# First layer's output projection in three fp32r passes with its weights split on GpSimd, and the second layer's gate products stacked

## The chip, the cores and the metric
One core of one Trainium2 chip runs the kernel. The time is the device time of one execution in microseconds (us); the number given is the median over runs. The profile is of one execution, taken by the hardware profiler.

## The reference
A decoder trunk of two layers on 1024 tokens of width 1024, in fp32. What matters here, cut down:

```python
def even_layer(...):                       # layer 0
    cq, ckv, k_rope, g_mla, u, g_s5 = split(x @ w_in)
    o_mla = mla_attention(cq, ckv, k_rope, ...) * silu(g_mla)     # (1024, 512), 8 heads, causal
    o_s5 = s5_layer(u, ...) * silu(g_s5)                          # (1024, 256); its last step is
                                                                  # y * sigmoid(y @ w_glu + b_glu)
    return concatenate([o_mla, o_s5]) @ w_out                     # (1024, 768) @ (768, 1024)

def odd_layer(...):                        # layer 1
    q, k, v, gk_low, g = split(x @ w_in)                          # gk_low: 16 columns
    log_a = log_sigmoid(gk_low @ w_gk2 + b_gk) / 16               # w_gk2: (16, 512)
    return (gated_linear_attention(q, k, v, log_a) * silu(g)) @ w_out

for each layer:
    x = layer_norm(4 ** 0.25 * x + layer(x))
```

## The kernel before, in words
All five instruction streams are written out by hand: `sync` (SP) issues every DMA in one queue, and GpSimd (POOL), ScalarE (ACT), VectorE (DVE) and TensorE (PE) each run their list in order and wait on semaphores. `PsumPlan` hands out the eight PSUM banks: `claim` waits until the bank's last job is drained, `filled` and `drained` wait for a job's completion by TensorE and by its reader. The helper `group` (L1588) issues one accumulation of matmuls, `turned` (L1597) transposes on TensorE.

Two kinds of product are in use. A plain fp32 product is one `matmul` call, which the profile shows as two MATMUL records. For the large products the operands are split into hi (the value rounded to fp32r) and lo (the value less hi, as fp32r), and `split_pairs` makes three fp32r passes of each product: hi·hi, hi·lo and lo·hi. Splitting costs a copy into hi and a subtraction into lo. For weights both are done on GpSimd (`split`, L884 and L885, through `wqk_split_head` and `slice_split_at`).

Layer 0 goes through its input projections, the S5 branch and then attention. Attention is 64 steps, one for each of 8 query tiles (i) and 8 heads (h), tile by tile (`attention_steps`, L458 on). In step n TensorE transposes the probabilities of head n (into "pt" banks), computes the scores of a later step (four ahead for i under 4, else two) and the value product of step n-1. VectorE copies the transposed probabilities (L595), takes the later step's row maximum (L1423) and, at tile ends, normalises the output of the tile and multiplies it with its gate (L1466 to L1472). ACT computes the exponentials (L1063). GpSimd rotates the queries of each later tile (L600 to L605). In steps 44 to 59 VectorE also runs the 16 pieces of the S5 branch's sigmoid (`sigmoid_gate`, L1441 on): add one, reciprocal, multiply into gs5. The glu products that they need are done before attention.

Then comes the output stage: for each token tile i, `output(i)` multiplies the tile's 768 mixed channels (4 blocks of OT, 2 of gs5) with w_out0 into z0, two halves of 512 columns, 6 fp32 products each. The first tile's product stands right behind the last value product in TensorE's queue, and the turning of tile 7 (OT 7) behind that. `layer_norm` (L1194 on) on VectorE adds the residual, takes the statistics and, after a square root on ACT (L1087), normalises; GpSimd multiplies and adds the two LayerNorm vectors (L907, L908); TensorE transposes the result (`x1_turned`) one tile later than its product, ACT writes x1T_hi (L1094) and VectorE x1T_lo (L1488). w_out0 is one DMA (L745) into a tile that is free by then.

Layer 1 begins with `low_rank(n)` (16 columns of the input projection, in 3 x 8 fp32r passes for each half of the tokens), the first query/key head `queries_keys(0)` between the two, then `gate_z(m)` (plain fp32, 16 rows deep) and the other query/key products. ACT copies the low-rank result to gkT (L1090, L1098). The weights of query/key heads 0 and 1 are loaded (L751) during attention, after the last sigmoid gate, and split on GpSimd before the output stage.

## Time and profile before

| | us |
|---|---|
| median of 3 runs | 928.06 (923.01 to 928.16) |
| the profiled execution, its own time | 926.22 |
| its span in the trace | 924.5 |
| TensorE busy in the span | 892.7 |
| VectorE busy | 448.1 |
| ScalarE busy | 273.7 |
| GpSimd busy | 222.0 |

Times of instructions in the rows are from the start of the span. A row of the timeline has the start, the time that the merged instructions cover, the engine, the line, the operation, its output and inputs, the shape and the count; in brackets how long the engine had been idle and what ended that. MATMUL records overlap, so the pitch between starts says more than the duration of one.

### The profile page before, as it was taken

To read this page: it belongs to the slowest core of one execution; us is meant where nothing else is said; L and a number is where in the kernel's file an instruction comes from. 1 tells how busy PE (TensorE), PEld (TensorE's weight loads), DVE (VectorE), ACT (ScalarE), POOL (GpSimd) and SP (SyncE) were. 2 spreads that over 40 slices of the span, in tenths; PEclk is the share of its full clock that TensorE was granted. 3 is DMA by queue.
4 is the path that set the end of the run, shared out by engine and by line. 5 is a ranking of instruction groups with operands and counts; after the bars stand their busy time and mean duration, and the time that the engine had idled before them with its cause. 6 is when DMAs were issued, how large, how long until landed. Compare 5 with 4: busy or idle time off the path is not lost. (4 is left out here: it accounts for less than half of the span.)

```text
span 924.5 us, 11820 instructions
## 1 busy us (share of the span) xinstructions
PE 892.7 (97%) x4384; PEld 691.5 (75%) x4384; DVE 448.1 (48%) x787; ACT 273.7 (30%) x536; POOL 222.0 (24%) x245
## 2 busy tenths in 40 slices
PE   7999999999999999999998999999999999999995
PEld 6888776766788777744455877888888888888884
DVE  5988689456666898344440433100000025554453
ACT  6152414553433344211113445002020326211120
POOL 2000002411110100544443230033413333142243
PEclk9999999999999999999999999999999999999998
DMA  9010255220000000522213110021001332021111
GB/s 338 11 28 23 72 84 121 85 76 2 1 1 1 1 1 13 170 77 83 91 57 103 46 46 1 11 86 52 23 23 50 98 114 92 23 81 57 46 48 67
DMA packets 34888, 55.61 MB, mean 60 GB/s; under 512 B 7664, under 2 KB 21232, under 8 KB 34816
## 3 DMA queue, kind: packets, MB, share of 16 engines
q1 hardware_dynamic: 34832, 54.87, 19.5%
q8 instruction: 35, 0.57, 0.3%
q14 instruction: 21, 0.17, 0.1%
HBM read 43.78 MB, written 9.44 MB: 58 GB/s over the span
## 5 line engine op out<-in xcount | busy, mean ns | idle before, releaser
L1521 DVE SCALAR_TENSOR_TENSOR w_out_lo<-w_out_raw,vecs,w_out_hi 128x1024 fp32r<-128x1024 f32 x8 | 10.5, 1314 | 161.8 <-ACT w_out_hi L1131 161.6
L1812 PEld LDWEIGHTS psum<-V,probT 128*128 128x128 f32 x576 | 69.3, 192 | 11.7 <-issue 8.1
L1812 PE MATMUL psum<-V,probT 128*128 128x64 f32 x576 | 74.4, 275 | 0.3 <-DVE rot L1468 0.3
L1675 PE MATMUL psum<-kT,qTt 96*128 96x512 f32 (+3 forms) x192 | 72.5, 487 | 1.2 <-DVE YT L612 1.2
L1063 ACT ACTIVATE prob<-psum,negmax 128x128 f32<-128x128 f32 (+7 forms) x64 | 47.4, 740 | 81.6 <-DVE negmax L1423 71.0
L1423 DVE TENSOR_REDUCE negmax<-psum 128x1 f32<-128x128 f32 (+7 forms) x64 | 48.5, 758 | 29.8 <-PE psum L1679 28.4
L1588 PE MATMUL psum<-w_out,OT 128*128 128x512 f32 x128 | 57.6, 593 | 0.0
L1588 PE MATMUL psum<-x1T_hi,wqk_hi 128*128 128x512 f32 x128 | 51.2, 400 | 0.0
L1588 PE MATMUL psum<-x1T_lo,wqk_hi 128*128 128x512 f32 x128 | 50.8, 397 | 0.0
L1588 PE MATMUL psum<-x1T_hi,wqk_lo 128*128 128x512 f32 x128 | 50.6, 395 | 0.0
L1588 PE MATMUL psum<-w_out_hi,Y1T_hi 128*128 128x512 f32 x128 | 50.6, 395 | 0.0
L1588 PE MATMUL psum<-w_out_hi,Y1T_lo 128*128 128x512 f32 x128 | 49.9, 390 | 0.0
L1588 PE MATMUL psum<-w_out_lo,Y1T_hi 128*128 128x512 f32 x128 | 49.8, 389 | 0.0
L1623 PE MATMUL psum<-wg_hi,x1T_lo 128*128 128x512 f32 x128 | 49.8, 389 | 0.0
L1623 PE MATMUL psum<-wv_hi,x1T_hi 128*128 128x512 f32 x128 | 49.8, 389 | 0.0
L1623 PE MATMUL psum<-wv_lo,x1T_hi 128*128 128x512 f32 x128 | 49.8, 389 | 0.0
L1623 PE MATMUL psum<-wv_hi,x1T_lo 128*128 128x512 f32 x128 | 49.8, 389 | 0.0
L1623 PE MATMUL psum<-wg_hi,x1T_hi 128*128 128x512 f32 x128 | 49.8, 389 | 0.0
L1623 PE MATMUL psum<-wg_lo,x1T_hi 128*128 128x512 f32 x128 | 49.8, 389 | 0.0
L595 DVE COPY probT<-psum 128x512 f32<-128x512 f32 (+3 forms) x64 | 37.8, 591 | 20.6 <-PE psum L1597 18.8
L1675 PEld LDWEIGHTS psum<-kT,qTt 96*128 96x128 f32 x192 | 32.4, 190 | 20.0 <-issue 16.8
L1588 PEld LDWEIGHTS psum<-w_out,OT 128*128 128x128 f32 x128 | 23.7, 190 | 26.8 <-issue 26.8
(349 smaller groups left out, 1923.7 us busy)
## 6 DMA issues: line engine op xcount, KB each, us to landing
wqk_raw<-odd_w_in_dram SPq DMA_DIRECT2D x8, 512.0 KB, 5.3
x_res<-x_dram SPq DMA_DIRECT2D x8, 512.0 KB, 3.4
x_scratch<-zn SPq DMA_DIRECT2D x8, 512.0 KB, 2.6
wv_raw<-odd_w_in_dram SPq DMA_DIRECT2D x16, 256.0 KB, 2.7
wg_raw<-odd_w_in_dram SPq DMA_DIRECT2D x16, 256.0 KB, 2.7
w_out_raw<-odd_w_out_dram SPq DMA_DIRECT2D x4, 1024.0 KB, 5.0
V<-x_scratch SPq DMA_DIRECT2D x8, 512.0 KB, 4.2
out_dram<-SG SPq DMA_DIRECT2D x8, 512.0 KB, 2.9
```

The lines of the kernel that those rows point to most:

```text
L595: ins = engine.activation(dst, src, ACT.Copy) if engine is nc.scalar else engine.tensor_copy(dst, src)
L1063: step.frees(act.activation(prob[:, place:place + (i + 1) * P], src, ACT.Exp, bias=negmax[:, n % 4:n % 4 + 1], accum_out=rsum[:, i % 2, h: ...
L1423: step(vec.tensor_reduce(negmax[:, n % 4:n % 4 + 1], scores(n)[0], AX_X, ALU.max, negate=True), max_set)
L1521: step(vec.scalar_tensor_tensor(w_out1[2][:, k, :], w_out1[0][:, k, :], gla_c[:, 4 + k % 2:5 + k % 2], w_out1[1][:, k, :].bitcast(F32), AL ...
L1588: mm = pe.matmul(out, lhsT, rhs, start=(k == 0), stop=(k == len(pairs) - 1))
L1623: mm = pe.matmul(bank(*job)[:, c0:c1], lhsT, rhs, start=(k == 0 and j == 0 and c0 == 0), stop=(k == KD - 1 and j == len(pairs) - 1), skip_ ...
L1675: mm = pe.matmul(psum[:, slot + part, 0:c1 - c0], qTt[:, i % 2, h, :], kT[:, h, c0:c1], start=True, stop=not diag, skip_group_check=diag)
L1812: mm = pe.matmul(bank("o", i)[:, h * VD:(h + 1) * VD], lhsT, rhs, start=(k == 0), stop=(k == len(pairs) - 1))
```

## The change
1. Output projection: w_out0 is loaded in six slices of 128 rows (1 to 3 after the S5 products y are done on TensorE, 4 and 5 after the last sigmoid gate, 0 after the last query rotation) and split on GpSimd: slices 1 to 3 behind the rotations of tiles 2, 3 and 4, the others behind the last rotation. The mixed channels are split too, tile by tile: ACT writes mix_hi, VectorE OT_lo and gs5_lo. `output(i)` makes three fp32r passes of each of its 12 products, and waits for the tile's low part.
2. The sigmoid gates move from steps 44 to 59 to steps 8 to 23.
3. Gate products: w_gk2 is laid out six times below itself (96 rows). `low_rank` uses hi and lo of its weight side by side (32 output rows, 16 matmuls instead of 24), ACT and VectorE write the result in six stacked parts (low_parts), and `gate_z` is one fp32r pass, 96 rows deep.
4. Query/key head 1 is loaded and split only after the output stage. x_res and zn have other places; the first slices of v1 wait until the last z0 is drained. Some unused semaphores go.

```diff
             plan.filled(sp, ("y", 3))
-            sp.dma_start(w_out0[:, :, :], even_w_out[0].rearrange("(k p) n -> p k n", p=P)).then_inc(w_out0_loaded, 16)
+            for k in range(1, 4):
+                w_out0_load(k, 0)
...
             sp.wait_ge(s5_states_set, 4)
+            sp.wait_ge(s5_out_set, 16)
+            for k in range(4, 6):
+                w_out0_load(k, 1)
             plan.filled(sp, ("q", NT - 1, 1))
-            sp.wait_ge(s5_out_set, 16)
+            sp.wait_ge(q_turned, NT)
+            w_out0_load(0, 2)
             wqk_load(0)
-            wqk_load(1)
...
             plan.filled(sp, ("z0", NT - 1, 1))
+            wqk_load(1)
+            plan.drained(sp, ("z0", NT - 1, 1))
...
# gpsimd, behind the rotation of query tile i
+                if 2 <= i < 5:
+                    w_out0_split_slice(i - 1, 0, 48)
...
+            for k in range(4, 6):
+                w_out0_split_slice(k, 1, 32)
+            w_out0_split_slice(0, 2, 16)
             pool.wait_ge(wgk_loaded, 16)
-            split(*(t[:, :, :] for t in w_gk), wgk_split)
-            for h in range(2):
-                wqk_split_head(h)
+            split(w_gk_raw[:, :, :], w_gk[:, :, 0:GR], w_gk[:, :, GR:2 * GR], wgk_split)
+            wqk_split_head(0)
...
                 step(pool.tensor_tensor(z, z, ln_gb[:, 1, :], ALU.add), x1_set)
+                if i == 1:
+                    pool.wait_ge(small_loaded, 16 * 3)
+                    step(pool.tensor_copy(gk2_parts[:, :], gk2[:, :]))
+                    step(pool.tensor_tensor(gk2_parts[4 * GR:6 * GR, :], gk2[4 * GR:6 * GR, :],
+                                            gk2_parts[4 * GR:6 * GR, :].bitcast(F32), ALU.subtract), gk2_split)
+            wqk_split_head(1)
...
# scalar; for tile 0 at the end of attention, for tile 1 behind it, for i + 2 behind the root of tile i
+            def mix_hi_tile(i):
+                cols = slice(i * P, (i + 1) * P)
+                plan.drained(act, ("OT", i))
+                if i == 0:
+                    act.wait_ge(s5_out_set, 16)
+                if i >= 2:
+                    plan.filled(act, ("z0", i - 2, 1))
+                step(act.activation(mix_hi[i % 2][:, 0:4, :], OT[:, :, cols], ACT.Copy))
+                step(act.activation(mix_hi[i % 2][:, 4:6, :], gs5[:, :, cols], ACT.Copy), mix_hi_set)
...
+            def low_hi(n):
+                s = slice(n * 512, (n + 1) * 512)
+                plan.filled(act, ("gk", n))
+                step(act.activation(low_parts[0:2 * GR, s], bank("gk", n)[0:2 * GR, :], ACT.Copy))
+                step(act.activation(low_parts[4 * GR:6 * GR, s], bank("gk", n)[0:2 * GR, :], ACT.Copy), low_hi_set)
...
# vector; for tile 0 behind tile 7's gate, for tile 1 behind OT 7, for i + 2 behind layer_norm of tile i
+            def mix_lo_tile(i):
+                cols = slice(i * P, (i + 1) * P)
+                vec.wait_ge(mix_hi_set, i + 1)
+                step(vec.tensor_tensor(OT_lo[:, :, cols], OT[:, :, cols], mix_hi[i % 2][:, 0:4, :].bitcast(F32),
+                                       ALU.subtract))
+                step(vec.tensor_tensor(gs5_lo[:, :, cols], gs5[:, :, cols], mix_hi[i % 2][:, 4:6, :].bitcast(F32),
+                                       ALU.subtract), mix_split)
+            def low_lo(n):
+                s = slice(n * 512, (n + 1) * 512)
+                vec.wait_ge(low_hi_set, n + 1)
+                step.frees(vec.tensor_tensor(low_parts[2 * GR:4 * GR, s], bank("gk", n)[0:2 * GR, :],
+                                             low_parts[0:2 * GR, s].bitcast(F32), ALU.subtract), ("gk", n))
...
-                    if 44 <= n < 60:
-                        sigmoid_gate(n - 44)
+                    if 8 <= n < 24:
+                        sigmoid_gate(n - 8)
...
# tensor
             def output(i):
                 if i == 0:
-                    pe.wait_ge(w_out0_loaded, 16)
-                    pe.wait_ge(s5_out_set, 16)
-                plan.drained(pe, ("OT", i))
+                    pe.wait_ge(w_out0_split, MIX // P)
+                pe.wait_ge(mix_split, i + 1)
...
-                          [(OT[:, k, ts] if k < 4 else gs5[:, k - 4, ts], w_out0[:, k, cs]) for k in range(6)])
+                          split_pairs([((mix_hi[i % 2][:, k, :], OT_lo[:, k, ts] if k < 4 else gs5_lo[:, k - 4, ts]),
+                                        (w_out0_hi[:, k, cs], w_out0_lo[k][:, cs])) for k in range(6)]))
...
-                group(("gk", n), bank("gk", n)[0:GR, :],
-                      split_pairs([([w[:, k, :] for w in w_gk[1:]], [x_[:, k, n * 512:(n + 1) * 512] for x_ in x1T])
-                                   for k in range(KD)]))
+                group(("gk", n), bank("gk", n)[0:2 * GR, :],
+                      [(w_gk[:, k, :], x_[:, k, n * 512:(n + 1) * 512]) for k in range(KD) for x_ in x1T])
...
-                group(("gate", m), bank("gate", m), [(gk2[:, h * P:(h + 1) * P], gkT[:, n * 512:(n + 1) * 512])])
+                group(("gate", m), bank("gate", m), [(gk2_parts[:, h * P:(h + 1) * P], low_parts[:, n * 512:(n + 1) * 512])])
```

## Rows read from the trace of the kernel before

**Rows 1.** The page, busy time, share of the span and instructions by engine:
```profile
PE 892.7 (97%) x4384; PEld 691.5 (75%) x4384; DVE 448.1 (48%) x787; ACT 273.7 (30%) x536; POOL 222.0 (24%) x245
```
**Rows 2.** Busy time by stretch, two stretches of attention; clock, DMA share, GB/s last:
```profile
204.60:240.10 35.50, 33.21 (x206) 24.12 (x206) 24.25 (x46) 12.84 (x38) 5.67 (x13) 1.00 0.00 1
305.00:368.00 63.00, 63.00 (x417) 48.74 (x416) 57.92 (x90) 24.77 (x48) 1.29 (x4) 1.00 0.00 1
```
**Rows 3.** Timeline of TensorE, output stage, x1's transposes before two neighbouring tiles:
```profile
441.70 1.04 PE L1597 MATMUL psum<-ident,zn 128*128 128x128 f32 x8
...
452.87 1.04 PE L1597 MATMUL psum<-ident,zn 128*128 128x128 f32 x8
```
**Rows 4.** Timeline of TensorE, first query/key product's first pass, and what follows its last:
```profile
481.66 0.40 PE L1588 MATMUL psum<-x1T_hi,wqk_hi 128*128 128x512 f32 x1
...
492.57 1.03 PE L1597 MATMUL psum<-ident,zn 128*128 128x128 f32 x8
```
**Rows 5.** Timeline of VectorE, one sigmoid gate's first operation and what follows the gate:
```profile
305.61 0.23 DVE L1446 TENSOR_SCALAR SGL<-SGL 128x128 f32<-128x128 f32 x1
...
307.18 0.96 DVE L1423 TENSOR_REDUCE negmax<-psum 128x1 f32<-128x768 f32 x1
```
**Rows 6.** A weight split on GpSimd, VectorE's gate product beside it, and that line's durations:
```profile
383.89 1.04 POOL L884 CAST wqk_hi<-wqk_raw 128x1024 fp32r<-128x1024 f32 x1
385.01 2.35 POOL L885 TENSOR_TENSOR wqk_lo<-wqk_raw,wqk_hi 128x1024 fp32r<-128x1024 f32 x1
...
386.42 1.49 DVE L1472 TENSOR_TENSOR gate<-gate,rot 128x512 f32<-128x512 f32 x1
...
L1472 DVE TENSOR_TENSOR gate<-gate,rot x8: 693/693/1490, 207.9 to 386.4; 128x512 f32<-128x512 f32 x8
```
**Rows 7.** Timeline, start and end of the output stage, VectorE and then TensorE:
```profile
385.32 0.20 DVE L1466 RECIPROCAL rinv<-rsum 128x8 f32<-128x8 f32 x1 [3.27 <-PE psum L1812]
...
396.85 0.69 DVE L1199 SCALAR_TENSOR_TENSOR zn<-x_res,psum 128x512 f32<-128x512 f32 x1
...
402.30 0.81 DVE L1206 TENSOR_SCALAR zn<-zn,stat 128x1024 f32<-128x1024 f32 x1
403.15 0.69 DVE L1199 SCALAR_TENSOR_TENSOR zn<-x_res,psum 128x512 f32<-128x512 f32 x1
...
408.11 1.09 PE L1597 MATMUL psum<-ident,zn 128*128 128x128 f32 x8 [1.79 <-POOL zn L908]
...
475.22 1.04 PE L1597 MATMUL psum<-ident,zn 128*128 128x128 f32 x8
```
**Rows 8.** Timeline, output stage, one tile on VectorE and then on GpSimd:
```profile
419.64 0.69 DVE L1199 SCALAR_TENSOR_TENSOR zn<-x_res,psum 128x512 f32<-128x512 f32 x1 [3.66 <-PE psum L1588]
...
421.23 0.21 DVE L1203 BATCH_NORM_AGGREGATE stat<-stat 128x2 f32<-128x12 f32 x1
...
423.08 1.42 DVE L1488 TENSOR_TENSOR x1T_lo<-psum,x1T_hi 128x512 fp32r<-128x512 f32 x2
...
423.19 2.35 POOL L907 TENSOR_TENSOR zn<-zn,ln_gb 128x1024 f32<-128x1024 f32 x1 [8.41 <-DVE zn L1206]
425.62 2.36 POOL L908 TENSOR_TENSOR zn<-zn,ln_gb 128x1024 f32<-128x1024 f32 x1
```
**Rows 9.** Timeline of TensorE and one row of ACT, low-rank and gate products:
```profile
476.02 0.48 PE L1588 MATMUL psum<-x1T_hi,w_gk_hi 128*16 128x512 f32 x1
...
495.66 0.39 PE L1588 MATMUL psum<-x1T_hi,w_gk_hi 128*16 128x512 f32 x1 [2.06 <-DVE x1T_lo L1488]
...
501.31 3.14 PE L1588 MATMUL psum<-gkT,gk 16*128 16x512 f32 x6
...
506.65 0.80 PE L1588 MATMUL psum<-x1T_hi,wqk_hi 128*128 128x512 f32 x1
...
554.88 1.98 PE L1588 MATMUL psum<-gkT,gk 16*128 16x512 f32 x4
...
501.48 0.59 ACT L1098 ACTIVATE gkT<-psum 16x512 f32<-16x512 f32 x1 [6.99 <-PE psum L1588]
```
**Rows 10.** Busy time by stretch, as in rows 2, where the granted clock is lower:
```profile
506.60:511.50 4.90, 4.90 (x12) 3.81 (x12) 1.27 (x2) 3.37 (x3) 0.00 (x0) 0.50 0.00 0
```

More of the change, by code:

```diff
@@ L175, in hybrid_trunk @@
         gk2_at = cursor[0]
-        gk2 = own("gk2", [GR, GKW])
+        gk2 = own("gk2", [6 * GR, GKW])
         o = cursor[0]
@@ L265, in hybrid_trunk @@
         OT = at("OT", RB + 7424, [P, H * VD // P, S])
-        w_out0 = at("w_out0", RB, [P, MIX // P, D])
+        OT_lo = at("OT_lo", RB + 7424, [P, H * VD // P, S], F32R)
+        gs5_lo = at("gs5_lo", D6, [P, 2, S], F32R)
+        mix_hi = [at(f"mix_hi{s}", (RD + 8192, D5)[s], [P, MIX // P, P], F32R) for s in range(2)]
+        w_out0_hi = at("w_out0_hi", RB, [P, MIX // P, D], F32R)
+        w_out0_at = (RB + 6144, RT, RT + 1024, D1 + 2048, D7, D7 + 1024)
+        w_out0_raw = [at(f"w_out0_raw{k}", o, [P, D]) for k, o in enumerate(w_out0_at)]
+        w_out0_lo = [at(f"w_out0_lo{k}", o, [P, D], F32R) for k, o in enumerate(w_out0_at)]
         SGL = at("SGL", D7, [P, 4, 512])
@@ L294, in hybrid_trunk @@
         cum = at("cum", RD + 19456, [P, 2, 512])
-        w_gk = split_pair("w_gk", E2 + 4096, [P, KD, GR])
-        ends = at("ends", E2 + 4096 + 2 * KD * GR, [P, GH, NCH])
+        w_gk_raw = at("w_gk_raw", E2 + 4096, [P, KD, GR])
+        w_gk = at("w_gk", E2 + 4096 + KD * GR, [P, KD, 2 * GR], F32R)
+        ends = at("ends", E2 + 4096 + 3 * KD * GR, [P, GH, NCH])
         resets = at("resets", RD + 12288, [P, 512])
-        two_ends = at("two_ends", E2 + 4096 + 2 * KD * GR + 64, [P, GH, NT])
-        assert (E2 + 4096 + 2 * KD * GR + 96) * 4 <= nc.sbuf_usable_end - base
+        two_ends = at("two_ends", E2 + 4096 + 3 * KD * GR + 64, [P, GH, NT])
+        assert (E2 + 4096 + 3 * KD * GR + 96) * 4 <= nc.sbuf_usable_end - base
         w_out1 = (at("w_out1_raw", RC, [P, KD, D]), at("w_out1_hi", RA, [P, KD, D], F32R),
@@ L340, in hybrid_trunk @@
         q_turned = sem("q_turned")
-        max_set, prob_set = sem("max_set"), sem("prob_set")
+        max_set = sem("max_set")
         gated = sem("gated")
-        w_out0_loaded, ln0_loaded = sem("w_out0_loaded"), sem("ln0_loaded")
+        w_out0_loaded, ln0_loaded = [sem(f"w_out0_loaded{s}") for s in range(3)], sem("ln0_loaded")
+        w_out0_split, mix_hi_set, mix_split = sem("w_out0_split"), sem("mix_hi_set"), sem("mix_split")
+        gk2_split, low_hi_set = sem("gk2_split"), sem("low_hi_set")
         xres_loaded = [sem(f"xres_loaded{s}") for s in range(2)]
@@ L870, in _, with split, w_out0_split_slice @@
                          s5_states_set if table is tabB else None)
+            def split(raw, hi, lo, signal):
+                step(pool.tensor_copy(hi, raw))
+                step(pool.tensor_tensor(lo, raw, hi.bitcast(F32), ALU.subtract), signal)
+            def w_out0_split_slice(k, batch, landed):
+                pool.wait_ge(w_out0_loaded[batch], landed)
+                split(w_out0_raw[k][:, :], w_out0_hi[:, k, :], w_out0_lo[k][:, :], w_out0_split)
             pool.wait_ge(s5_n2_set, 4)
@@ L880, in _ @@
                            q_turned)
-            def split(raw, hi, lo, signal):
-                step(pool.tensor_copy(hi, raw))
-                step(pool.tensor_tensor(lo, raw, hi.bitcast(F32), ALU.subtract), signal)
+                if 2 <= i < 5:
+                    w_out0_split_slice(i - 1, 0, 48)
             def wqk_split_head(h):
@@ L1077, in _ @@
                     scaled_queries(*n)
+                elif what == "z0":
+                    mix_hi_tile(0)
                 elif what == "pt":
@@ L1087, in _ @@
                     step(act.activation(stat[:, 20:21], stat[:, 1:2], ACT.Sqrt, bias=eps[:, 0:1]), root_set)
+                if i + 2 < NT:
+                    mix_hi_tile(i + 2)
                 if i == NT:
-                    plan.filled(act, ("gk", 0))
-                    step.frees(act.activation(gkT[:, 0:512], bank("gk", 0)[0:GR, :], ACT.Copy), ("gk", 0))
+                    low_hi(0)
                 if i:
@@ L1096, in _ @@
                              x1_hi_set)
-            plan.filled(act, ("gk", 1))
-            step.frees(act.activation(gkT[:, 512:1024], bank("gk", 1)[0:GR, :], ACT.Copy), ("gk", 1))
+            low_hi(1)
             for h in range(GH + 1):
@@ L1288, in _ @@
             step(vec.tensor_tensor(LR[:, :, :], LR[:, :, :], e4[0], ALU.add))
-            step(vec.tensor_scalar(tabA[:, :, :], tabA[:, :, :], 1.0, None, ALU.add), s5_powers_set)
+            step(vec.tensor_scalar(tabA[:, :, :], tabA[:, :, :], 1.0, None, ALU.add))
             slice_lo("ina", 4)
@@ L1472, in _ @@
                     step(vec.tensor_tensor(gate[:, i, :], gate[:, i, :], rot[:, 0, :], ALU.mult), gated)
+                elif what == "z0":
+                    mix_lo_tile(0)
                 elif what == "OT":
@@ L1483, in _ @@
                     layer_norm(zn[:, i % 2, :], x_res[:, i % 2, :], "z0", i, i)
+                if i + 2 < NT:
+                    mix_lo_tile(i + 2)
                 if i:
@@ L1956 @@
     }
-    for name in ("mla_w_uq", "mla_w_ukv", "s5_w_glu", "even_w_out", "odd_w_in", "gla_w_gk2", "odd_w_out"):
+    laid_out["gla_w_gk2"] = np.tile(given["gla_w_gk2"][0], (6, 1))
+    for name in ("mla_w_uq", "mla_w_ukv", "s5_w_glu", "even_w_out", "odd_w_in", "odd_w_out"):
         laid_out[name] = given[name]
```

25 lines of the change are left out of this document (15 added, 10 removed).

## The prediction
> **What bounds the kernel now.** I read the page first, then TensorE's timeline and groups, then the same stretches on VectorE (DVE), ScalarE (ACT) and GpSimd (POOL). TensorE is the bound nearly throughout: 892.7 of 924.5 us busy [rows 1]. So what leaves its queue shortens the kernel, as long as no other engine takes over. Two stretches decide whether one does. In 305 to 368 us VectorE is 92% busy (57.92 of 63 us), and TensorE still has no gap [rows 2]: the sigmoid gates of the S5 branch sit there now and cost TensorE nothing. In 204.6 to 240.1 us (attention steps 8 to 23, where the gates go) VectorE has 24.25 of 35.5 us busy in 46 instructions [rows 2]: it looks half idle, but the steps are short. In the output stage TensorE runs one tile every 11.17 us (441.70 to 452.87), 0.87 of that transposes and 10.30 the products [rows 3].
>
> **Output projection, on TensorE.** One fp32 product appears as two records, and a tile has 12 products: 10.30/12 = 0.858 us each [rows 3]. The fp32r pitch is in the query/key products: 48 of them between 481.66 and 492.57, 0.227 us each [rows 4]. Three passes cost 0.68 us, so a tile falls to 12 x 0.68 = 8.18, plus 0.87 is 9.05 instead of 11.17 us. For eight tiles TensorE alone would give back 17.0 us.
>
> **The moved sigmoid gates.** One gate holds VectorE from 305.61 until the next operation at 307.18, 1.57 us [rows 5]; sixteen are 25.1 us. In their new place VectorE has 35.5 - 24.25 - 46 x 0.035 us between instructions (from 403.11 to 403.15, for one [rows 7]) = 9.6 us free. It runs in order, and its copy of the transposed probabilities is what the next value product waits for; behind each gate are queued that step's maximum (then the exponential, the next transposes) and the next copy. TensorE can run ahead by a step, not by sixteen. So 25.1 - 9.6 = 15.5 us comes onto the path. Bounds: 0 if all were hidden, 25.1 if none of the free time could be used; I take 15.5, because once VectorE has a backlog its short waits for TensorE go away. Taking the gates out of 305 to 368 gives nothing, since TensorE had no gap there.
>
> **Six weight splits on GpSimd.** Each is a cast of 1.04 and a subtraction of 2.35 us [rows 6]. GpSimd has the time; the three after query tiles 2 to 4 end long before the next rotation, and slices 4, 5 and 0 and the first query/key head fall at 306 to 330, before 385. What they cost is VectorE's time. The gate product of 128x512 took 1.49 us at 386.42, beside a subtraction that ran until 387.36; its median over eight is 0.693 [rows 6]. An operation with two SBUF inputs evidently waits until GpSimd's is over. The last multiplication of a sigmoid gate is of that kind, and there is one per 3.2 us (51 us over 16 steps): a subtraction meets one with 2.35/3.2 and holds it 1.2 us on average, the cast adds 0.17. Three splits: 3.2 us, and 0.3 for the query rotations. Bounds 0 and 3 x 3.39 = 10.2. I take 3.5; attention then grows by 19.0 us.
> The Trainium skill (SBUF — State Buffer, Who interferes with whom) says more than the row shows: tensor_scalar with one SBUF source can enter a two-port mode that takes the same lock, and the first to start holds it for the whole instruction. The gate's "+1" would then wait too. By the row the term is 3.5; by the rule about 2 us more. No row shows a tensor_scalar blocked, so it stays out of the sum.
>
> **The start of the output stage.** Now the first output follows the last value product at once, and tile 7's normalising runs beside it. With the change it waits for the low part of tile 0, which stands on VectorE behind tile 7's normalising. VectorE starts at 385.32 [rows 7]; reciprocal 0.31, product 0.79 and gate 0.73 (GpSimd is free now), then two subtractions, 0.73 and 0.42 (by 0.69 for 512 columns), end at 388.3. TensorE idles 3.3 us. Output 0 ends at 396.6, the turned tile 7 is copied by 398.0, tile 1's low part follows at 399.15: output 1 waits 2.2 us more. Normalising tile 0 took 396.85 to 403.11; from 399.15 it ends at 405.4. GpSimd's two operations follow (4.9 us, and 1.0 of blocking, below), so the first transposes of x1 start at 411.4 instead of 408.11 [rows 7].
>
> **The tiles after it.** VectorE does per tile: half a normalisation (1.59, from 419.64 to 421.23), a second half of 3.44 (419.64 to 423.08), and two x1 low parts, 1.42 and a gap [rows 8]. That was 6.5 of 11.17 us. New are two subtractions with two SBUF inputs, right where GpSimd starts on the tile (423.19) [rows 8]. The first (0.72) is ahead of GpSimd and delays it by 0.6; the second waits for GpSimd's first 2.35 us operation and then delays its second by 0.4. So mix_lo costs 0.72 + 2.35 + 0.43 = 3.5 us, VectorE's tile is 1.59 + 3.44 + 3.5 + 1.45 = 10.0, and that is more than TensorE's 9.05. Tile 1's normalising, started at 409.0, ends at 414.05, and each further tile 10.0 later: tile 6 at 464.05, its transposes 4.9 later at 469.0. Before, they started at 475.22 [rows 7]: the whole stage, start included, gains 6.2 us. Bounds: 10.6 at TensorE's own pace (411.4 less 1, then 6 x 9.05), and a loss of 3.3 if the pace stayed at 11.17.
>
> **The gate products.** The low-rank product falls from 24 to 16 matmuls of 0.233 us, twice (5.64 us for 24, from 476.02 to 481.66 [rows 4, 9]): 3.7 us. The four gate products after the second one run from 501.31 to 506.65, 5.34 us [rows 9]. In their place: two copies on ACT (0.59 each), one subtraction on VectorE (0.69), with handovers 2.4 us before the second product, and ACT must empty both banks for products 3 and 4: 3.9 us, 1.4 less. The four later ones cost 0.86 each (554.88, two in 1.9 us) [rows 9], now 0.23: 2.5. Together 7.6 us (bounds: 6.2 with no gain at the first four, 9.5 with all at pitch). The split of the 96-row weight (about 2 us) lies in GpSimd's gap after tile 1. The second query/key head now loads only after tile 7's x1 (477.4): 4 us of queue, 5 to land, 7 to split is 493.6, and its first product is due at about 506. This cover is 12 us wide.
>
> **TensorE's clock.** The granted clock is 1.00 in the attention stretches [rows 2], and 0.50 from 506.6 to 511.5 [rows 10], the lower level of 1.2 GHz, after 2.06 us idle before 495.66, narrow products and waits [rows 9]. There 12 products took 0.43 instead of 0.23 us, 2.4 us in all. I expect that one to stay. The new 3.3 us idle before output 0 may bring another: half of 2.4 is 1.2 us. Bounds 0 and 11.9: at the lower clock all through the starved stretch, its 33.2 us of TensorE work [rows 2] would take 66.4, against the 54.5 that VectorE needs.
>
> **Sum.** 19.0 - 6.2 - 7.6 + 1.2 = +6.4 us, on the profiled execution's own 926.22 (span 924.5 and 1.7 around it): 932.6 us. The median of the runs shown is 928.06, 1.8 above it; measured medians may stand as much higher.
>
> **The rivals.**
> (a) VectorE hides the gates, because 24.25 busy of 35.5 us [rows 2] leaves a third free. Then the change is faster: 926.2 - 6.2 - 7.6 + 1.2 = 913.6. Against it: 25.1 does not go into 9.6 us. It decides if VectorE's idle time in the stretch exceeds 25 us. Chance 0.07.
> (b) The blocking between VectorE and GpSimd is dear only by accident at 386 us; without it attention grows 15.5, and the output stage runs at TensorE's pace and gains 10.6: 926.2 + 15.5 - 10.6 - 7.6 + 1.2 = 924.7. For it: one blocked row only. Chance 0.17.
> (c) The clock falls in the starved stretch, where TensorE has work for 33 of 54 us. Work at half speed fills the gaps, and after a filled stretch the clock came back at 511.5, so I take half of the 11.9 us: 938.6. Against it: the same steps with less waiting run at 1.00 now. Chance 0.13.
> (d) The output stage keeps its old pace, because each tile waits for VectorE, ACT, VectorE, GpSimd in turn: 926.2 + 19.0 + 3.3 - 7.6 + 1.2 = 942.1. Against it: from the second half's start at 419.64 to x1 at 427.98 is 8.4 us [rows 8], under 9. Chance 0.11.
> My own forecast has 0.52, with 928 to 938 as its range.
>
> **How the numbers follow.** Time 932.6. The range takes in (b) and the two slower ones: 922 to 943. A measurement of this kernel can tell about 1% (9 us) from no change. Faster by more than that is (a), 0.07. Slower by more, over 935.5, is (c), (d) and a fifth of mine: 0.35. The rest, 0.58, is within 1%.
>
> **What would show it.** In the profile after: 16 reciprocals of 128x128 between 205 and 262 us, VectorE over 90% busy there, step 24 starting 17 to 22 us later than 240.1; some gate multiplications far over 0.29 us, one of 1.2 or more per split; TensorE idle 3 us before the first output; the output stage's period at 10.0 us, TensorE idle 1 us per tile on x1 or mix_lo; 32 low-rank matmuls; attention's end at about 404. I am wrong if step 24 starts before 250, if the period is 9.05, or if TensorE's clock leaves 1.00 before 385.

## The result, and the profile after

The kernel after takes 939.25 us (median of four runs, 936.33 to 943.81), the kernel before in the same job 927.27. The ratio is 1.0143, with a 95% interval of 0.0052 either way (1.0091 to 1.0195): slower by 1.4%. The forecast was 932.6 us with a range of 922 to 943, so the time lies inside, 6.65 us above the likeliest value. The profiled execution took 938.81 us, its span 937.1 against 924.5.

The page of the kernel after, its busy times and the granted clock in 40 slices:

```profile
PE 882.4 (94%) x4456; PEld 716.0 (76%) x4456; DVE 481.9 (51%) x805; ACT 283.4 (30%) x554; POOL 251.7 (27%) x259
...
PEclk9999999997699999999999899999999999999998
```

TensorE is busy 10.3 us less than before [rows 1], and the kernel is longer: it was made to wait. Two slices in the tenth and eleventh place stand at 7 and 6. That is attention, where the gates now are. Busy time by stretch there (from, to, length, then TensorE, its weight loads, VectorE, ScalarE, GpSimd, and the granted clock):

```profile
204.60:262.00 57.40, 43.24 (x201) 29.54 (x200) 48.27 (x86) 11.87 (x36) 15.78 (x19) 0.76 0.00 1
...
212.00:216.00 4.00, 1.99 (x4) 1.17 (x4) 3.76 (x8) 0.00 (x0) 0.00 (x0) 0.50 0.00 0
```

Before, TensorE was busy 33.21 of 35.5 us at 1.00 here [rows 2]. Now it has 43.24 of 57.4 at a mean of 0.76, and in 212 to 216 half of the time at 0.50 (1.2 GHz). Where it waits, TensorE's waits of the whole kernel (total, times, longest, us):

```profile
PE psum L1668 <- DVE qTt L1466: 9.3, 4, 3.4
...
PE psum L1883 <- DVE probT L602: 4.9, 4, 3.0
PE psum L1659 <- issue: 3.2, 1, 3.2
```

A line names the waiting engine and its line, and behind the arrow who ended the wait. The turned queries (qTt) and the turned probabilities (probT) are VectorE copies that stand behind a gate in its queue. The line "issue, 3.2" is the start of the output stage. TensorE's timeline from the last value product on (start, length, and in brackets the idle time before and who ended it):

```profile
407.91 3.68 PE L1883 MATMUL psum<-V,probT 128*128 128x64 f32 x32
...
414.76 0.47 PE L1659 MATMUL psum<-w_out_hi,mix_hi 128*128 128x512 f32 x1 [3.17 <-issue]
...
427.29 0.50 PE L1659 MATMUL psum<-w_out_hi,mix_hi 128*128 128x512 f32 x1 [2.04 <-DVE gs_lo L1505]
...
439.07 1.09 PE L1668 MATMUL psum<-ident,zn 128*128 128x128 f32 x8 [1.71 <-POOL zn L932]
...
467.20 1.09 PE L1668 MATMUL psum<-ident,zn 128*128 128x128 f32 x8 [0.43 <-POOL zn L932]
...
476.92 1.09 PE L1668 MATMUL psum<-ident,zn 128*128 128x128 f32 x8 [0.44 <-POOL zn L932]
...
495.88 1.09 PE L1668 MATMUL psum<-ident,zn 128*128 128x128 f32 x8
```

Before, the value product of the same kind started at 381.55 and the first output at 385.06, 3.5 later; in the kernel after an output could have started at 411.4. The later tiles go 9.72 us apart (467.20 to 476.92), not 11.17 [rows 3]. The low-rank and gate products:

```profile
496.73 0.48 PE L1659 MATMUL psum<-x1T_hi,w_gk 128*32 128x512 f32 x1
...
500.50 0.40 PE L1659 MATMUL psum<-x1T_hi,wqk_hi 128*128 128x512 f32 x1
...
520.48 0.83 PE L1659 MATMUL psum<-low_parts,gk_parts 96*128 96x512 f32 x2 [1.90 <-DVE low_parts L1511]
...
522.47 0.63 PE L1659 MATMUL psum<-x1T_hi,wqk_hi 128*128 128x512 f32 x1
```

So the 12.6 us between the two spans go as follows.

| stretch | before | after | difference | forecast |
|---|---|---|---|---|
| to the end of attention (the first output could start) | 385.06 | 411.4 | +26.4 | +19.0 |
| from there to the transposes of tile 6 | 90.16 (to 475.22) | 84.5 (to 495.88) | -5.7 | -6.2 |
| from there to the query/key product behind the first gate products | 31.43 (to 506.65) | 26.59 (to 522.47) | -4.8 | -5.1 |
| the rest of the span | 417.85 | 414.63 | -3.2 | -2.5 |

The clock term of +1.2 has no stretch of its own. One term is wrong by 7 us, the three others by at most 0.7.

### The profile page after: what moved, and what is told of

Its sections match the earlier page's. It is cut to its first block and busy times, and to the rows that moved or that the text cites. A ratio compares the mean times of both kernels' runs of the same rounds, so it can differ in the third digit from the quotient of the medians.

```text
span 937.1 us, 12044 instructions
## 1 busy us (share of the span) xinstructions
PE 882.4 (94%) x4456; PEld 716.0 (76%) x4456; DVE 481.9 (51%) x805; ACT 283.4 (30%) x554; POOL 251.7 (27%) x259
## 5 line engine op out<-in xcount | busy, mean ns | idle before, releaser
L1592 DVE SCALAR_TENSOR_TENSOR w_out_lo<-w_out_raw,vecs,w_out_hi 128x1024 fp32r<-128x1024 f32 x8 | 10.3, 1285 | 162.1 <-ACT w_out_hi L1180 161.9
L1883 PEld LDWEIGHTS psum<-V,probT 128*128 128x128 f32 x576 | 71.9, 198 | 18.5 <-issue 8.5
L1883 PE MATMUL psum<-V,probT 128*128 128x64 f32 x576 | 77.1, 281 | 5.2 <-DVE probT L602 4.9
L1746 PE MATMUL psum<-kT,qTt 96*128 96x512 f32 (+3 forms) x192 | 75.7, 505 | 1.2 <-DVE YT L619 1.2
L931 POOL TENSOR_TENSOR zn<-zn,ln_gb 128x1024 f32<-128x1024 f32 x8 | 21.8, 2726 | 110.0 <-DVE zn L1255 110.0
L1659 PE MATMUL psum<-w_out_hi,mix_hi 128*128 128x512 f32 x96 | 39.4, 410 | 5.2 <-issue 3.2
```

The costliest lines, as they stand in the source:

```text
L931: step(pool.tensor_tensor(z, z, ln_gb[:, 0, :], ALU.mult))
L1592: step(vec.scalar_tensor_tensor(w_out1[2][:, k, :], w_out1[0][:, k, :], gla_c[:, 4 + k % 2:5 + k % 2], w_out1[1][:, k, :].bitcast(F32), AL ...
L1659: mm = pe.matmul(out, lhsT, rhs, start=(k == 0), stop=(k == len(pairs) - 1))
L1746: mm = pe.matmul(psum[:, slot + part, 0:c1 - c0], qTt[:, i % 2, h, :], kT[:, h, c0:c1], start=True, stop=not diag, skip_group_check=diag)
L1883: mm = pe.matmul(bank("o", i)[:, h * VD:(h + 1) * VD], lhsT, rhs, start=(k == 0), stop=(k == len(pairs) - 1))
```

## The experiments

All times are medians beside runs of the kernel before on the same chip (925.5 to 927.5 us in the four jobs).

**The gates back in their old steps.**

```
-                    if 8 <= n < 24:
-                        sigmoid_gate(n - 8)
+                    if 44 <= n < 60:
+                        sigmoid_gate(n - 44)
```

> The change with the sigmoid gates back in steps 44 to 59. Theory (the gates in the short steps are what costs): attention ends again near 385 us instead of 411.4, everything else of the change stays, so 939.25 less 26 is 913 us, faster than before by 1.5%. Rival (the output stage or the splits carry the loss): at most 5 us come back, 934 us. Slices 4, 5 and 0 of the weights now load after 366 us and take 10.5 us of GpSimd, so they are ready at about 382; if they are late, the first output waits longer than 3.2 us.

Measured: 917.18 us (915.87 to 918.28), ratio 0.9902 (0.988 to 0.9925). The rest of the change gains 8.3 us, so the move of the gates alone turns a faster kernel into a slower one. It missed 913 by 4 us. Attention ended 1.6 us later than in the kernel before (the last value product at 383.18 against 381.55), with the granted clock at 0.59 in 210 to 214 us. The larger part is behind it, on VectorE's timeline:

```profile
387.26 0.69 DVE L1531 TENSOR_TENSOR rot<-psum,rinv 128x512 f32<-128x512 f32 x1
388.05 1.50 DVE L1535 TENSOR_TENSOR gate<-gate,rot 128x512 f32<-128x512 f32 x1
389.59 1.41 DVE L1503 TENSOR_TENSOR OT_lo<-OT,mix_hi 128x512 fp32r<-128x512 f32 x1
391.03 2.44 DVE L1505 TENSOR_TENSOR gs_lo<-gs,mix_hi 128x256 fp32r<-128x256 f32 x1
```

The slices 4, 5 and 0 can only load once the gates are done, and the first query/key head follows them on GpSimd, whose splits then run until 393.2. The three operations with two SBUF inputs take 5.35 us where the kernel after needs 1.8 (0.69, 0.69, 0.42), and TensorE sat idle 6.72 us before the first output, not 3.17. The operation on PSUM (rot) is not held. Moving the gates forward has this one advantage: GpSimd is done with its splits before the output stage.

**The gates alone, in the kernel before.**

```
-                    if 44 <= n < 60:
-                        sigmoid_gate(n - 44)
+                    if 8 <= n < 24:
+                        sigmoid_gate(n - 8)
```

> The kernel before with nothing changed but the gates' place, steps 8 to 23. Theory: VectorE's order costs 15.5 us and TensorE's clock, which falls when it is starved, another 5 or so: 927.3 + 20 = 947 us, between 942 and 950, with granted clock under 1.00 between 205 and 262 us. Rival without a clock loss: 943 us and a clock of 1.00. Rival in which VectorE hides the gates: 927 us.

Measured: 948.95 us (947.36 to 950.79), ratio 1.0247 (1.022 to 1.0273). The first output came at 409.91 instead of 385.06: the gates cost 24.85 us of the 25.1 that they take on VectorE. Busy time by stretch in this run:

```profile
204.60:240.10 35.50, 24.42 (x121) 17.03 (x118) 30.38 (x60) 6.49 (x20) 2.74 (x6) 0.79 0.00 1
```

VectorE has 30.38 of 35.5 us where it had 24.25, not all of it: it waits too. Its waits for TensorE came to 7.7 us from 204.6 us to the last gate, and to 10.0 us in the same steps of the kernel before (204.6 to 240.1), so on balance only 2.3 us of them were used up. Three of its waits on the row maximum (negmax), each in or right behind a stretch at half clock:

```profile
216.39 0.42 DVE L1423 TENSOR_REDUCE negmax<-psum 128x1 f32<-128x256 f32 x1 [1.55 <-PE psum L1679]
...
244.76 0.56 DVE L1423 TENSOR_REDUCE negmax<-psum 128x1 f32<-128x384 f32 x1 [1.72 <-PE psum L1679]
...
273.70 0.69 DVE L1423 TENSOR_REDUCE negmax<-psum 128x1 f32<-128x512 f32 x1 [3.32 <-PE psum L1679]
```

In the kernel before the same three maxima waited 1.29, 1.24 and 1.18 us, with the clock at 1.00. The runs with shorter gates below show what the clock has to do with it. Where VectorE hardly waited before, the gates cost nearly their length at full clock too: the way from the maximum at 219.98 to that at 231.52 took 11.54 us for 5.94 before (214.42 to 220.36), so four gates, 6.3 us of work, added 5.6.

**The splits away from the gates**, in the kernel after: slices 1 to 3 are split behind the last rotation.

```
-                if 2 <= i < 5:
-                    w_out0_split_slice(i - 1, 0, 48)
...
+            for k in range(1, 4):
+                w_out0_split_slice(k, 0, 48)
```

> The change with all six weight splits behind the last query rotation, so that none lies beside a sigmoid gate. Theory (an operation with a shared port waits for GpSimd): the long gate operations (1.47, 2.18 and 1.34 us) are gone, 3 to 5 us less, 935 us. Rival (the clock and VectorE's order are all): the same 939 us.

Measured: 934.72 us (934.22 to 936.67), ratio 1.0096 (1.0072 to 1.012), 4.5 under the kernel after. The first and the last of the gates' three lines, kernel after (count, then shortest, median and longest in ns):

```profile
L1495 DVE TENSOR_SCALAR SGL<-SGL x16: 226/227/2180, 205.4 to 264.5; 128x128 f32<-128x128 f32 x16
...
L1497 DVE TENSOR_TENSOR gs<-gs,SGL x16: 291/292/1471, 206.8 to 265.8; 128x128 f32<-128x128 f32 x16
```

And in this run:

```profile
L1495 DVE TENSOR_SCALAR SGL<-SGL x16: 226/226/229, 205.6 to 258.3; 128x128 f32<-128x128 f32 x16
...
L1497 DVE TENSOR_TENSOR gs<-gs,SGL x16: 291/292/509, 206.8 to 259.6; 128x128 f32<-128x128 f32 x16
```

The long ones are gone. The last value product started at 404.46 instead of 407.91, so the blocking is worth about 3.4 us and the gates with the rest of attention 23.0. Both are from one profile each, and runs with the same attention code differ by up to 2 us there (384.42 to 386.62 in the three runs with early parts below).

**The score products of steps 12 to 27 issued twice**, in the kernel after.

```
+                    for _ in range(2 if 12 <= n < 28 else 1):
+                        mm = pe.matmul(psum[:, slot + part, 0:c1 - c0], qTt[:, i % 2, h, :], kT[:, h, c0:c1],
...
```

> The change with the score matmuls of steps 12 to 27 issued twice (the second overwrites the first), which gives TensorE 9 to 10 us more work in the stretch where it is starved. Theory (the fallen clock costs about 6 us there): the clock stays at 1.00 for more of the stretch and attention ends no later, 936 us, between 933 and 939, in spite of the added work. Rival (the low clock lies in TensorE's idle time and costs nothing): 939 to 941 us whatever the clock does. Rival (TensorE is not starved): 948 us.

Measured: 936.27 us (933.81 to 937.04), ratio 1.01 (1.0071 to 1.0129): about 10 us of work added to the engine that is the bound elsewhere, and the kernel is no slower, with a mean clock of 0.85 for 0.76 in 204.6 to 262. Its last value product started 1.7 us earlier, at 406.20. The median is 3 us lower, but the two ratios to the kernel before overlap (up to 1.0129, and from 1.0091), so a gain is not shown. The rival that the added work costs its full length (948 us) is out.

**Three issues of the score products**, in the kernel before with the gates in steps 8 to 23.

```
+                    for _ in range(3 if 8 <= n < 24 else 1):
+                        mm = pe.matmul(psum[:, slot + part, 0:c1 - c0], qTt[:, i % 2, h, :], kT[:, h, c0:c1],
...
```

> The kernel before with the gates in steps 8 to 23 (as in the run with the gates alone, 948.95 us), and the score products of the same steps issued three times into the same bank: 17 us of useless TensorE work (8 steps of 0.86 and 8 of 1.28 us) exactly where TensorE starves. If the granted clock is part of the cost of the gates, TensorE now has 33 + 17 = 50 us of work for some 54 us of VectorE's, keeps 1.00, and the first output product comes at 403 to 406 us instead of 409.9: 942 to 945 us, faster with more work. Rival, that the 24.8 us are VectorE's own work and waits and the clock takes nothing: the first output product at 410 or later and 949 us or more.

Measured: 953.46 us (953.17 to 955.81), ratio 1.0308. The expectation failed: the clock stayed near 1.00 up to 262 us, and the first output came at 412.15, 2.2 us later than with the gates alone. Busy time by stretch:

```profile
204.60:240.00 35.40, 32.19 (x168) 23.72 (x168) 28.03 (x58) 7.63 (x24) 2.74 (x6) 0.95 0.00 1
240.00:262.00 22.00, 20.21 (x111) 13.78 (x110) 17.88 (x33) 5.23 (x14) 2.77 (x6) 1.00 0.00 1
```

VectorE has less done in 204.6 to 240 than with the gates alone (28.03 against 30.38). The useless products stand between the queries and the maximum, and up to the same step VectorE waited 12.9 us for score products, in ten pieces (9.7 in six without the added ones). Filling TensorE put in a new wait. It can be followed where the clock was 1.00: the maxima at 248.19 and 252.48 waited 0.95 and 1.17 us. Before, they waited 1.24 and 1.45; less a gate of 1.57, plus 1.3 for the added issues, that makes 0.97 and 1.18. Without the added issues nothing would be left of these waits. Behind the last gate the clock fell here too (0.50 in 268 to 272 us). So this run doesn't price the clock by its total.

**Shorter gates, alone**: the kernel before with the gates in steps 8 to 23, and the reciprocal over 64 and then over 8 of 128 columns. The edit for 64:

```
-                step(vec.reciprocal(SGL[:, k, s], SGL[:, k, s]))
+                step(vec.reciprocal(SGL[:, k, s][:, 0:64], SGL[:, k, s][:, 0:64]))
```

> The kernel before with the gates in steps 8 to 23, with the reciprocal of each gate over 64 of its 128 columns; the other 64 columns of each gate are left without it. A gate then holds VectorE about 1.12 us and not 1.57 (half of 0.953 less), sixteen 17.9 us. With whole gates attention grew by 24.8 us. If VectorE's 9.6 us of free time are used first (the prediction's way), it grows by 17.9 - 9.6 = 8.3 us, the first output product at 393.4. If no free time is used, it grows by 17.9 to 403, about 942 us. If the clock falls only where TensorE starves much, the growth lies under 8.3 + 6 = 14.3, at 393 to 399.

> As the run with half reciprocals, with the reciprocal over 8 of 128 columns, the other 120 left without it. A gate is then 1.57 - 0.953 + 0.20 = 0.82 us (0.20 is VectorE's 128x8 reciprocal of the row sums), sixteen 13.1 us. Free time used first: attention grows by 13.1 - 9.6 = 3.5 us, first output product at 388.6, about 929 us. No free time used: 13.1, at 398, about 938 us. The two short-gate runs and the whole-gate run together give the slope: 1 us per us of gate work with an offset of 9.6, or without one, or steeper than 1 where the clock falls.

Measured: 942.95 us with 64 columns, 937.82 with 8 (two timed runs each, before 927.49). TensorE's last value product (381.55 before) with 64 columns:

```profile
397.36 3.68 PE L1812 MATMUL psum<-V,probT 128*128 128x64 f32 x32
```

And with 8:

```profile
392.26 3.68 PE L1812 MATMUL psum<-V,probT 128*128 128x64 f32 x32
```

The reciprocals took 0.553 and 0.203 us, so sixteen gates are 18.7 and 13.1 us of VectorE.

Attention grows by 15.8 and 10.7 us for them, and by 24.85 for the 25.1 of whole gates. On balance 0.25 to 2.9 us of the 9.6 us of free time were used. Two neighbouring steps show why it was so few. VectorE's maxima in the kernel before, where the clock is 1.00:

```profile
228.57 0.56 DVE L1423 TENSOR_REDUCE negmax<-psum 128x1 f32<-128x384 f32 x1 [1.24 <-PE psum L1679]
...
231.58 0.56 DVE L1423 TENSOR_REDUCE negmax<-psum 128x1 f32<-128x384 f32 x1 [1.45 <-PE psum L1679]
```

The same two with 64 columns, then TensorE's query products in front of them, then the granted clock there:

```profile
241.07 0.56 DVE L1423 TENSOR_REDUCE negmax<-psum 128x1 f32<-128x384 f32 x1 [2.05 <-PE psum L1679]
...
244.07 0.56 DVE L1423 TENSOR_REDUCE negmax<-psum 128x1 f32<-128x384 f32 x1 [0.27 <-PE psum L1679]
...
236.72 2.92 PE L1588 MATMUL psum<-w_uq,cT 128*128 128x384 f32 x4 [0.45 <-DVE qTt L1417]
...
241.81 1.46 PE L1588 MATMUL psum<-w_uq,cT 128*128 128x384 f32 x4
...
237.00:240.80 3.80, 3.80 (x7) 1.79 (x7) 1.89 (x5) 1.03 (x3) 0.00 (x0) 0.50 0.02 4
241.40:245.00 3.60, 3.60 (x23) 2.71 (x22) 2.42 (x6) 1.58 (x4) 0.91 (x2) 1.00 0.01 2
```

At full clock the gate of 1.17 us fits into the wait whole: 1.45 - 1.17 is 0.28, and 0.27 are left. With 8 columns the gate is 0.82, and 0.63 are left of the same wait. At half clock the product that the maximum waits for takes 2.92 us for 1.46, and the wait is 2.05 us in spite of the gate. So free time of this kind is usable while the clock is 1.00, and the fall of the clock takes it back.

An estimate of how much, from VectorE's rows: of each wait, what is longer than the wait before less the gate (or, on the copies of the probabilities and behind the last gate, than the wait before).

| gate work | attention grows by | of it longer waits at or behind half clock | rest | work less 9.6 |
|---|---|---|---|---|
| 13.1 | 10.7 | 4.5 | 6.2 | 3.5 |
| 18.7 | 15.8 | 4.8 | 11.0 | 9.1 |
| 25.1 | 24.85 | 8.5 | 16.3 | 15.5 |

With whole gates the 8.5 are 1.55, 0.32, 1.72 and 1.25 us on four maxima, 0.61 and 0.92 on two copies, and 2.14 (3.32 less 1.18) behind the last gate. The rest comes within 0.8 to 2.7 us of the forecast's rule.

**The gate products alone, in the kernel before** (the core of the edit):

```
-                group(("gate", m), bank("gate", m), [(gk2[:, h * P:(h + 1) * P], gkT[:, n * 512:(n + 1) * 512])])
+                group(("gate", m), bank("gate", m), [(gk2_parts[:, h * P:(h + 1) * P], low_parts[:, n * 512:(n + 1) * 512])])
```

> The kernel before with the gate-product part alone: the low-rank product in 16 stacked fp32r matmuls, the eight gate products with 96 rows in fp32r. The profile after has 4.8 us less from the x1 transposes of tile 6 to the first query/key pass, and 3.2 us less behind it, of which 2.5 are the four later gate products. If that is the part's own worth: 925.5 - 8 = 917.5 us (916 to 919). Rival, that what is behind the first pass is only waited for elsewhere: 925.5 - 4.8 = 920.7 us.

Measured: 918.6 us (917.48 to 919.9), ratio 0.9916 (0.9897 to 0.9935): 7.6 us less than before, where the forecast's term was 7.6.

**The first two tiles' parts made inside attention.** The kernel after, with the gates at other steps, and ScalarE's and VectorE's parts of tiles 0 and 1 in steps 58 to 61.

```
+                    if n in (58, 59):
+                        plan.filled(act, ("qT", NT - 1, 1))
+                        mix_hi_tile(n - 58)
...
+            GATE_STEPS = [32, 34, 36, 38, *range(40, 52)]
...
+                    if n in GATE_STEPS:
+                        sigmoid_gate(GATE_STEPS.index(n))
+                    if n in (60, 61):
+                        mix_lo_tile(n - 60)
```

> The kernel after with the gates at other steps (32, 34, 36, 38 and 40 to 51) and the high and low parts of output tiles 0 and 1 made inside attention: the high parts by ScalarE in steps 58 and 59, the low parts by VectorE in steps 60 and 61. Compared with the run that had the gates back in 44 to 59 (917.2 us): its idle of 6.7 us before the first output product and of 2.0 before the second go, and with them the stretch at half clock after them, some 2 us. Expected 917.2 - 8.7 - 2 = 906.5 us, up to 910 where the low parts fall beside a GpSimd split. Rival, that the idle only moves on to the x1 transposes of tile 0, which wait for LayerNorm anyway: 914 to 916 us.

Measured: 908.8 us (908.15 to 909.6), ratio 0.9811 (0.9793 to 0.9828): faster than both kernels, 17 us under before. The first output follows the last value product at once, at 388.23, with no idle time:

```profile
384.74 3.68 PE L1883 MATMUL psum<-V,probT 128*128 128x64 f32 x32
...
409.68 1.27 PE L1668 MATMUL psum<-ident,zn 128*128 128x128 f32 x8 [4.37 <-POOL zn L932]
...
449.19 1.09 PE L1668 MATMUL psum<-ident,zn 128*128 128x128 f32 x8 [0.44 <-POOL zn L932]
...
458.90 1.09 PE L1668 MATMUL psum<-ident,zn 128*128 128x128 f32 x8 [0.43 <-POOL zn L932]
```

The gates were not free here either: with the clock at 1.00 throughout 204.6 to 385 us, attention ended 3.2 us later than in the kernel before (384.74 against 381.55). The rival had a share: of the 6.7 + 2.0 us of idle time of the run with the gates back, 1.1 moved on to the first x1 transposes, where the wait grew from 3.25 to 4.37.

**Low parts between the two halves of LayerNorm**, on that kernel.

```
                     for n in range(2):
+                    if n and between:
+                        between()
...
-                if i + 2 < NT:
-                    mix_lo_tile(i + 2)
```

> The run with early parts of tiles 0 and 1, with one thing moved: VectorE makes the low parts of output tile i+1 between the two halves of LayerNorm of tile i (i from 1 to 6), not those of tile i+2 behind it, so that the two mixes don't meet GpSimd's scale and shift. If it is the lock between VectorE and GpSimd (0.42 us became 2.5) that sets the pace of 9.7 us per tile, the pace is 9.1 to 9.5 and the time 2 to 3 us under the run with early parts. Rival, that TensorE's 9.05 us per tile and the order of its queue set the pace: within 1 us of it. A loss of more than 2 us would say that the later statistics are the longer chain.

Measured: 910.02 us (906.63 to 912.28), within 1.3 of the run before it, so no gain is shown. The pace did fall, from 9.71 to 9.46 us:

```profile
440.28 1.09 PE L1669 MATMUL psum<-ident,zn 128*128 128x128 f32 x8
...
449.74 1.09 PE L1669 MATMUL psum<-ident,zn 128*128 128x128 f32 x8
```

Over the four tiles from 431.14 to 468.66 that is 0.9 us. The low parts did not get out of GpSimd's way: gs_lo went from 2.50 back to 0.42 us, but OT_lo took 1.9 for 0.69, beside GpSimd's second operation. Attention in front of it ended 1.9 us later than in its parent, with the same code up to there: the granted clock was 0.59 in 210 to 214 us, and 1.00 in the parent. That scatter hides a gain of this size.

**Without GpSimd's scale and shift.**

```
-                step(pool.tensor_tensor(z, z, ln_gb[:, 0, :], ALU.mult))
-                step(pool.tensor_tensor(z, z, ln_gb[:, 1, :], ALU.add), x1_set)
+                step(pool.tensor_tensor(z[:, 0:8], z[:, 0:8], ln_gb[:, 0, 0:8], ALU.mult))
+                step(pool.tensor_tensor(z[:, 0:8], z[:, 0:8], ln_gb[:, 1, 0:8], ALU.add), x1_set)
```

> The run with early parts of tiles 0 and 1, with GpSimd's scale and shift of the first LayerNorm cut to 8 of 1024 columns, so that the other 1016 columns of x1 are left without them. With no GpSimd operation of 2.35 us beside it, the gate row of the low parts should take 0.42 us in every tile, the pace of the output stage should be TensorE's own 9.05 us, and the first x1 transposes come some 5 us earlier (two operations of 2.35). If the pace is 9.7 us by the lock, the run gains about 4 + up to 5 = 5 to 9 us on the run with early parts; if the lock has no part in the pace, only the 5 us at the start, less where they are hidden behind output products.

Measured: 901.94 us (two timed runs), 6.9 under its parent, the span 8.5 less. VectorE's and TensorE's rows of one tile:

```profile
427.86 0.42 DVE L1505 TENSOR_TENSOR gs_lo<-gs,mix_hi 128x256 fp32r<-128x256 f32 x1
...
432.43 1.03 PE L1668 MATMUL psum<-ident,zn 128*128 128x128 f32 x8
...
441.48 1.03 PE L1668 MATMUL psum<-ident,zn 128*128 128x128 f32 x8
```

The pace is 9.05 us, as worked out for TensorE alone, and gs_lo takes 0.42. The first x1 transposes come 4.5 us earlier (405.19) and those of tile 6 8.5 earlier (459.59 against 468.12): 4.0 us of pace. So GpSimd's two operations are what keeps this stage above TensorE's pace. How much of it is their length and how much the blocking, this edit does not tell, since it takes away both.

**The gates in steps 36 to 51**, on the kernel with early parts.

```
-            GATE_STEPS = [32, 34, 36, 38, *range(40, 52)]
+            GATE_STEPS = [*range(36, 52)]
```

> The run with early parts of tiles 0 and 1 (908.8 us) with the gates in steps 36 to 51, not 32, 34, 36, 38 and 40 to 51. That run has 1.4 us of TensorE waiting for turned queries between 255 and 310 us, and 18.64 of 20 us busy in 280 to 300. If the early gates cause it, the gates in 36 to 51 give 1 to 2 us back: 907 to 908. Rival, that TensorE runs short in the denser row of sixteen gates: 908.8 or more.

Measured: 913.58 us (911.8 to 915.07), ratio 0.9868. The guess was wrong: TensorE waited 2.3 us for turned queries in 250 to 312 us, and 1.4 in its parent, and attention ended 0.9 us later. But 4.7 us were lost in the span. The larger part is not in the gates at all; the last section shows it.

## Why the prediction was right and where it failed

**The gates (15.5 us forecast, 23 to 25 measured).** This term is the one that was mis-sized. It took VectorE's 9.6 us between instructions as usable, and on balance 0.25 to 2.9 us of them were. The rule itself holds roughly: at full clock the gates went into VectorE's long waits whole (1.45 to 0.27 and 0.63 us), and without the waits that grew at half clock 16.3 us are left of the 24.85. What failed is the premise that TensorE's clock stays at 1.00 there. A gate ahead of a copy makes TensorE wait, its clock falls, and its next products hold VectorE up for longer than before. The kernel after shows both: TensorE waits 9.3 and 4.9 us for VectorE in the list of waits, and VectorE still waits in turn. The maximum in this row waited 1.29 us before:

```profile
217.76 0.42 DVE L1472 TENSOR_REDUCE negmax<-psum 128x1 f32<-128x256 f32 x1 [1.21 <-PE psum L1750]
```

The upper bound in the text, 25.1 "if none of the free time could be used", came nearer to the number than the 15.5. VectorE is 84% busy in the stretch (48.27 of 57.4), not over 90% as the forecast's own sign had it.

**The clock (1.00 before 385 forecast; 0.76 in 204.6 to 262 measured).** This is the step that failed: the sum has 1.2 us for the clock and nothing of it in attention. The text named a fall there as what would make it wrong, and rival (c) as the case, at 0.13. That rival's 938.6 us is within 0.2 us of the profiled run, and its mechanism is what the rows show. Its size, 6 us, was half of a bound; the count above gives 8.5 us for the run with the gates alone, and 5.4 us in the kernel after (1.21, 1.72 and 1.20 on maxima, 0.92 on a copy, 0.35 behind the last gate), where 26.4 less 5.4 and 3.4 for the splits leaves 17.6 for the 15.5. These are estimates from single waits. No run held the clock at 1.00 with nothing else changed: the score products issued twice brought it from 0.76 to 0.85 and cost nothing for 10 us of work, those issued three times brought a wait of their own.

The measured time lies above 928 to 938, the range of the forecast's own mechanism, and in the outcome "over 935.5", which had 0.35 against 0.58 for less than 1%. It lies inside 922 to 943 because that range took in (c) and (d). The other terms came out nearly as worked out, so no errors cancelled.

**The splits on GpSimd (3.5 us forecast, about 3.4 measured).** Right in size, within a scatter of 2 us; but the forecast had only gate multiplications held, so part of the agreement is luck. In the kernel after, two tensor_scalars of 0.23 us took 2.18 and 1.34 (the second at 257.62), and one multiplication 1.47 us: 1.95 and 1.1 us more on the additions, and 1.2 on the multiplication. VectorE and then GpSimd, at the same time:

```profile
224.94 2.18 DVE L1495 TENSOR_SCALAR SGL<-SGL 128x128 f32<-128x128 f32 x1
```

```profile
224.69 2.34 POOL L891 TENSOR_TENSOR w_out_lo<-w_out_raw,w_out_hi 128x1024 fp32r<-128x1024 f32 x1
```

The tensor_scalar starts 0.25 us behind GpSimd's subtraction and ends with it. The Trainium skill (SBUF — State Buffer, Who interferes with whom) says that this form can take the lock shared with GpSimd, and that the first to start has it for the whole instruction; the forecast left that out as not shown, and these rows show it.

**The start of the output stage (idle 3.3 and 2.2 us forecast, 3.17 and 2.04 measured).** Right, step by step. The first x1 transposes came 27.7 us after the end of attention, not 26.3: behind each of the two idle times the granted clock was near 0.50 for 3 us (415 to 418.4 and 428.8 to 432). In the first, nine products took 0.43 us each for 0.23, which held back the rest of the first output by about 1.8 us. The second cost nothing, since TensorE then waited 1.71 us for x1. The clock term of 1.2 us stood for this.

**The pace (10.0 us forecast, 9.1 to 9.7 measured, mean 9.47).** The mechanism is right. VectorE and GpSimd in the kernel after:

```profile
451.94 0.69 DVE L1503 TENSOR_TENSOR OT_lo<-OT,mix_hi 128x512 fp32r<-128x512 f32 x1
...
452.66 2.50 DVE L1505 TENSOR_TENSOR gs_lo<-gs,mix_hi 128x256 fp32r<-128x256 f32 x1
```

```profile
452.05 2.84 POOL L931 TENSOR_TENSOR zn<-zn,ln_gb 128x1024 f32<-128x1024 f32 x1 [2.67 <-DVE zn L1255]
```

The low parts took 3.2 us of VectorE for 3.5 forecast, GpSimd's operation 2.84 for 2.35, and the cut to 8 columns brought the pace to 9.05. The blocking came in full, as forecast: gs_lo took 2.50 us in all six tiles, and from the third on they came 9.7 us apart, for 10.0 forecast. TensorE's first two pitches and its last were shorter (9.13, 9.28 and 9.25), since it hardly had to wait there. The stage gained 5.7 us for 6.2.

**The gate products (7.6 us forecast; 7.6 alone, 8.0 in the kernel after).** Right. The low-rank product takes 3.77 us (496.73 to 500.50) for 5.64, twice, and the wait before the second gate product is the 1.90 above.

**The rivals.** (a) is refuted by the gates alone, (b) by the longer rows, and (d) by the pace; (c) is the one that the rows bear out. That the same change with the gates left at 44 to 59 is faster (917.2) was not a rival and would have been worth the sentence.

## What to carry to other kernels

Where two engines wait for each other inside every step, the idle time of VectorE is room only while TensorE keeps its clock. Work in front of TensorE's next operand makes it wait, its clock can fall, and the waits that were to hide the work grow: 13 to 25 us of work cost 82 to 99% of their length here. Look for a stretch where TensorE has no gap, as it had none where the gates stood. Before work is moved, look at what hides it where it stands; here the same work was free in steps 44 to 59 and cost 23 to 25 us in steps 8 to 23. Low parts that the next stage needs first belong in front of the stage's boundary, and a VectorE operation with two SBUF inputs can be held until the GpSimd operation that it meets is over (0.42 us became 2.50 here).

## What was not expected of the hardware

The granted clock can fall or not after the same waits. Behind the second gate product the kernel with early parts and its sibling with the gates in 36 to 51 run the same code. Busy time by stretch of the first:

```profile
494.00:501.00 7.00, 6.86 (x30) 5.75 (x31) 1.35 (x2) 5.32 (x5) 6.57 (x7) 1.00 0.00 0
```

And of the second:

```profile
494.00:501.00 7.00, 5.85 (x13) 4.20 (x14) 1.14 (x3) 6.56 (x8) 6.57 (x6) 0.55 0.00 0
```

Both waited 1.90 us for the low parts (492.72 and 494.65), then 0.70 and 0.50 for ScalarE. From the fourth gate product to the next pair the first took 22.08 us (494.14 to 516.22), the second 24.52 (496.34 to 520.86): 2.4 us by the clock alone. The same holds at the first x1 transposes, where eight took 1.27 us in the one (409.68) and 1.97 in the other (410.54) behind waits of 4.37 and 4.36. A difference of 2 to 3 us between two kernels of this family can be this and nothing else.

In attention of the kernel after the granted clock was 0.50 (1.2 GHz) in 212 to 216 us, behind a wait of 2.90 us for turned queries that ended at 209.16, and the same query product took 2.93 us at 214.11 and 1.46 at 218.16. Useless products in such a place are not always a loss: 10 us of them cost nothing in the kernel after, but 17 us of them, put between the queries and the maximum in the kernel with the gates alone, cost 4.5.
